# Hybrid decoder layer, input projection: token sums on the vector engine, the rotary turn on GpSimd

## What is computed

```
z = x @ w_in + b_in              # 2048 x 1024 by 1024 x 2240 (parts in the order of the kernel)
# the rotary turn, on the first quarter of each head's columns (16 of 64, or 8 of 32):
x1, x2 = head[:half], head[half:rot]      # half = 8 or 4
x1' = x1*cos - x2*sin ;  x2' = x2*cos + x1*sin
```

## Time and profile before

| | |
|---|---|
| median of 3 runs | 3696.45 us (3692.97 to 3696.48) |
| profiled execution, span from first to last instruction | 3696.2 us |
| mean granted clock of PE | 0.969 |
| PE busy | 3464.1 us (94%) |
| DVE busy | 2404.9 us (65%) |
| ACT busy | 1793.5 us (49%) |
| POOL busy | 1237.3 us (33%) |

### The profile page before, as it was taken

One profiled execution on the slowest core, in us unless ns is written; L12 is line 12 of the kernel. 1 busy time (PEld: TensorE's weight loads), 2 busy tenths in 40 slices (PEclk: granted clock), 3 DMA queues, 4 the chain that ended last, 5 costly groups with the idle time before them and its releaser, 6 DMA issues. The chain is left out here.

```text
span 3696.2 us, 55781 instructions
## 1 busy us (share of the span) xinstructions
PE 3464.1 (94%) x19082; PEld 2965.1 (80%) x19082; DVE 2404.9 (65%) x4983; ACT 1793.5 (49%) x3056; POOL 1237.3 (33%) x1944
## 2 busy tenths in 40 slices
PE   6999978899999999999999899799999999999998
PEld 6999867777888878878878788588888788888876
DVE  9999556667676766676774355756654657665354
ACT  3323235677776777677767333433333333333232
POOL 5454124544443333333222033432321425322021
PEclk9999899899999999999999999899999999999999
DMA  4344310000000000000000245332224442322444
GB/s 146 114 150 146 101 33 24 17 17 24 17 17 10 17 16 9 10 15 5 7 9 27 81 141 155 128 124 79 92 83 171 159 169 77 110 99 89 140 137 171
DMA packets 189701, 289.63 MB, mean 78 GB/s; under 512 B 33395, under 2 KB 129779, under 8 KB 189427
## 3 DMA queue, kind: packets, MB, share of 16 engines
q1 hardware_dynamic: 185300, 285.11, 23.4%
q10 hardware_dynamic: 4128, 1.05, 0.1%
HBM read 211.15 MB, written 74.97 MB: 77 GB/s over the span
## 5 line engine op out<-in xcount | busy, mean ns | idle before, releaser
L1674 ACT ACTIVATE shared<-a_ps_st 128x512 f32<-128x512 f32 x716 | 437.6, 615 | 285.9 <-PE a_ps_st L1560 146.9
L2785 PE MATMUL f_ps<-f_x_four,f_w_hi 128*128 128x512 f32 x1408 | 437.9, 392 | 11.5 <-DVE f_w_lo L2923 11.5
L2785 PE MATMUL f_ps<-f_x_three,f_w_hi 128*128 128x512 f32 x1056 | 325.4, 389 | 1.6 <-DVE f_w_lo L2923 1.6
L2785 PEld LDWEIGHTS f_ps<-f_x_four,f_w_hi 128*128 128x128 f32 x1408 | 266.5, 190 | 68.3 <-DVE f_w_lo L2923 13.1
L1584 PEld LDWEIGHTS a_ps_o<-a_vsl,shared 128*128 128x128 f32 x2176 | 295.5, 200 | 19.3 <-DVE a_fin L1891 0.7
L1382 POOL TENSOR_SCALAR a_tk<-a_tk,a_halves 128x1 f32<-128x1 f32 x336 | 107.0, 318 | 584.1 <-ACT a_junk_a L1681 582.5
L1584 PEld LDWEIGHTS a_ps_o<-a_dv,shared 128*128 128x128 f32 x2176 | 285.9, 194 | 12.0
L1584 PE MATMUL a_ps_o<-a_vsl,shared 128*128 128x65 f32 x2176 | 287.0, 277 | 0.0
L1584 PE MATMUL a_ps_o<-a_dv,shared 128*128 128x65 f32 x2176 | 276.9, 271 | 0.0
L2785 PE MATMUL f_ps<-f_x_four,f_w_lo 128*128 128x512 f32 x704 | 275.8, 392 | 0.0
L294 PE MATMUL p_ps<-pw_hi,px_hi 128*128 128x384 f32 (+1 forms) x672 | 227.9, 339 | 47.3 <-DVE pw_lo L399 29.9
(11 more groups left out here) (372 smaller groups left out, 8905.6 us busy)
## 6 DMA issues: line engine op xcount, KB each, us to landing
shared<-in_w_down SPq DMA_DIRECT2D x88, 512.0 KB, 3.5
px_raw<-in_x_t SPq DMA_DIRECT2D x48, 512.0 KB, 4.6
shared<-in_w_gate SPq DMA_DIRECT2D x44, 512.0 KB, 5.0
shared<-in_w_up SPq DMA_DIRECT2D x44, 512.0 KB, 4.8
g_scratch<-shared SPq DMA_DIRECT2D x22, 1024.0 KB, 7.6
shared<-g_scratch SPq DMA_DIRECT2D x88, 256.0 KB, 3.6
z_scratch<-p_z SPq DMA_DIRECT2D x16, 768.0 KB, 3.4
o_scratch<-a_oacc SPq DMA_DIRECT2D x32, 256.0 KB, 2.1
```

The lines of the kernel that those rows point to most:

```text
L1674: act.activation(p_t[:, s % PT_RING, :], ps_st[s % ST_BANKS][:, :], ACT.Exp, scale=SCALE).then_inc(exp_done, 1)
L2785: mm = pe.matmul(out[:, :], w[:, j, k * P:(k + 1) * P], x_part(j, x)[:, k], start=(k == 0 and i == 0), stop=(k == 3 and i == 2))
```

## The change

The sums of the token blocks of sets 0 and 1 stay on POOL; from set 2 on they are made by DVE, with the same operands, spread over DVE's list: in set `N`, sum 1 of set `N+1` behind slot 0, sum 3 of set `N+1` behind slot 3, sums 0 and 2 of set `N+2` behind slots 5 and 6. Their order within a set changes from 0, 1, 2, 3 to 0, 2, 1, 3, and ACT waits on a new semaphore `sv_done` for them. The rotary turn leaves DVE. POOL makes it for both token tiles of a set at once, in place: two products with `sin` into `rb`, a product with `cos` in `zt` itself (one operation in the first two passes, two in the last), and the sum. To give it operands of few dimensions, the cosines are kept twice side by side (`cos8`) for the heads of 64 and once (`cos4`) for the heads of 32, so ACT makes five tables in place of three. `z_ready` counts one a set in place of two. Small buffers are laid over others, `ra` is gone.

```diff
+        def x_sums(eng, N, k, done, at):
+
+            if k == 3:
+                eng.wait_ge(x_lo_done, SEVEN * N + 2)
+            elif N:
+                eng.wait_ge(x_lo_done, SEVEN * (N - 1) + (4, 3, 7)[k])
+            if k == 0:
+                for half in range(2):
+                    eng.wait_ge(x_ld[2 * (N % 2) + half], 16 * (N // 2 + 1))
+                op = eng.tensor_tensor(s_block(0), x_block(N, 1, 0), x_block(N, 1, 1), ALU.add)
...
         @block.gpsimd
         def _(pool):
...
+            def rope(N):
+
+                a, p = divmod(N, PAIRS_Q)
+                heads, dim, f, fo = ROPES[a]
+                done = 3 * N
+                if N == 0:
+                    pool.wait_ge(trig_done, 5)
+                pool.wait_ge(sum_done, SEVEN * N + 7)
+                if N:
+                    pool.wait_ge(z_ready, N)
+                zr = zt[:, N % 2, :, 0:heads * dim].rearrange("p i (h d) -> p i h d", h=heads)[:, :, :, 0:2 * f]
+                qb = rb[:, :, 0:heads, 0:2 * f]
+                first, second = slice(0, f), slice(f, 2 * f)
+                for m, (dst, src) in enumerate(((first, second), (second, first))):
+                    sn = sin2[:, 2 * p:2 * p + 2, m, fo:fo + f].unsqueeze(2).broadcast_to([P, 2, heads, f])
+                    pool.tensor_tensor(qb[:, :, :, dst], zr[:, :, :, src], sn, ALU.mult).then_inc(turned, 1)
+                pool.wait_ge(turned, done + 2)
+                if fo:
+                    cs = cos4[:, 2 * p:2 * p + 2].unsqueeze(2).broadcast_to([P, 2, heads, f])
+                    pool.tensor_tensor(zr[:, :, :, first], zr[:, :, :, first], cs, ALU.mult)
+                    pool.tensor_tensor(zr[:, :, :, second], zr[:, :, :, second], cs, ALU.mult).then_inc(turned, 1)
+                else:
+                    cs = cos8[:, 2 * p:2 * p + 2].rearrange("p t a f -> p t (a f)").unsqueeze(2).broadcast_to([P, 2, heads, 2 * f])
+                    pool.tensor_tensor(zr, zr, cs, ALU.mult).then_inc(turned, 1)
+                pool.wait_ge(turned, done + 3)
+                pool.tensor_tensor(zr, zr, qb, ALU.add).then_inc(z_ready, 1)
...
             for N in range(NS):
                 a, p = divmod(N, PAIRS_Q)
-                if N + 1 < NS:
-                    x_sums(N + 1)
+                if N == 0:
+                    for k in range(4):
+                        x_sums(pool, 1, k, s_done, 4)
+                if N:
+                    rope(N - 1)
                 if a + 1 < PASSES and 2 <= p <= 5:
                     w_sums(pool, a + 1, p - 2, (t12_done, t12_done, t34_done, t34_done)[p - 2])
+            rope(NS - 1)
...
-                    if j == 1 and N:
-                        rope(N - 1, 0)
-                rope(N, 1)
-            rope(NS - 1, 0)
+                    if j == 0 and 2 <= N + 1 < NS:
+                        x_sums(dve, N + 1, 1, sv_done, 4 * (N - 1))
+                    if j == 3 and 2 <= N + 1 < NS:
+                        x_sums(dve, N + 1, 3, sv_done, 4 * (N - 1))
+                    if j >= 5 and N + 2 < NS:
+                        x_sums(dve, N + 2, (0, 2)[j - 5], sv_done, 4 * N)
```

More of the change, by code:

```diff
@@ L105, in projection_phase @@
         zt = sb("p_z", [P, 2, 2, 2 * WMAX])
[L106 to L109, removed]
+        posi, posf, freq = uu[:, 2, 0:TILES].bitcast(I32), uu[:, 1, 0:TILES], uu[:, 1, TILES:TILES + 12]
+        cos8 = sb("p_cos8", [P, TILES, 2, 8])
+        cos4 = sb("p_cos4", [P, TILES, 4])
         sin2 = sb("p_sin", [P, TILES, 2, 12])
-        ra = sb("p_ra", [P, 12, 2, 8])
-        rb = sb("p_rb", [P, 12, 2, 8])
+        rb = sb("p_rb", [P, 2, 12, 16])
         bank = [ctx.enter_context(nc.psum_tensor(f"p_ps{c}", [P, 512], F32)) for c in range(8)]
@@ L127, in projection_phase @@
         s_done = sem("p_s_done")
+        sv_done = sem("p_sv_done")
         t12_done = sem("p_t12_done")
@@ L143, in projection_phase @@
         z_ready = sem("p_z_ready")
+        turned = sem("p_rope")
         z_out = [sem(f"p_z_out{b}") for b in range(2)]
@@ L205, in store @@
                 a, p = divmod(N, PAIRS_Q)
-                sp.wait_ge(z_ready, 2 * (N + 1))
+                sp.wait_ge(z_ready, N + 1)
                 sp.dma_start(z_rows[:, 2 * p:2 * p + 2, OFFSETS[a]:OFFSETS[a] + 2 * WIDTHS[a]], zt[:, N % 2, :, 0:2 * WIDTHS[a]]).then_inc(z_out[N % 2], 16)
@@ L240, in _ @@
                 sp.wait_ge(z_out[u], 16 * (NS // 2))
+        def x_sums(eng, N, k, done, at):
[7 more added lines that the diff above has]
+                op = eng.tensor_tensor(s_block(0), x_block(N, 1, 0), x_block(N, 1, 1), ALU.add)
+            elif k == 1:
+                op = eng.tensor_tensor(s_block(2), x_block(N, 0, 0), x_block(N, 1, 0), ALU.subtract)
+            elif k == 2:
+                eng.wait_ge(done, at + 1)
+                op = eng.tensor_tensor(s_block(1), s_block(0), x_block(N, 0, 0), ALU.subtract)
+            else:
+                eng.wait_ge(done, at + 3)
+                op = eng.tensor_tensor(s_block(1), x_block(N, 0, 1), s_block(1), ALU.subtract)
+            op.then_inc(done, 1)
@@ L267, in _ @@
             pool.memset(ones[:, :].bitcast(F32), 1.0).then_inc(bias_clear, 1)
-            x_sums(0)
+            for k in range(4):
+                x_sums(pool, 0, k, s_done, 0)
             for n in (2, 3):
@@ L310, in high_x @@
                     act.wait_ge(x_ld[2 * (N % 2) + (j > 0)], 16 * (N // 2 + 1))
+                elif N < 2:
+                    act.wait_ge(s_done, 4 * N + {3: 1, 2: 2, 1: 3, 6: 4}[j])
                 else:
-                    act.wait_ge(s_done, 4 * N + {3: 1, 2: 2, 1: 3, 6: 4}[j])
+                    act.wait_ge(sv_done, 4 * (N - 2) + {3: 1, 1: 2, 2: 3, 6: 4}[j])
                 act.activation(slot(x_hi, j), x_source(N, j), ACT.Copy).then_inc(x_hi_done, 1)
@@ L334, in _ @@
                     act.wait_ge(trig, 1)
-                    act.activation(cos1[:, :, :], rr[:, 1], ACT.Sin).then_inc(trig_done, 1)
+                    for m in range(2):
+                        act.activation(cos8[:, :, m, :], rr[:, 1, :, 0:8], ACT.Sin).then_inc(trig_done, 1)
+                    act.activation(cos4[:, :, :], rr[:, 1, :, 8:12], ACT.Sin).then_inc(trig_done, 1)
                     act.activation(sin2[:, :, 0, :], rr[:, 0], ACT.Sin, scale=-1.0).then_inc(trig_done, 1)
@@ L411, in summed @@
                     dve.wait_ge(first_kept, N + 1)
+                    if N:
+                        dve.wait_ge(sum_done, s0)
                     op = dve.tensor_tensor(u2, m1, piece, ALU.add)
@@ L421, in summed @@
                         dve.wait_ge(z_out[u], 16 * (N // 2))
-                    if N == 0:
-                        dve.wait_ge(trig_done, 3)
                     op = dve.tensor_tensor(zt[:, u, 1, w:2 * w], u3, piece, ALU.add)
@@ L432, in summed @@
                 op.then_inc(sum_done, 1)
[L434 to L452, removed]
             dve.wait_ge(bias_in, 32)
```

## The result

The changed kernel takes 3673.64 us (median of 4 runs, 3666.94 to 3678.91), the kernel before 3694.71 in the runs beside them (3692.89 to 3696.48); with the 3696.45 that stood before the prediction, that is 21 to 23 us less. The ratio is 0.9937, 95% interval 0.9924 to 0.995. The time lies in the range, 3 us under the forecast of 3677. Single executions of one kernel differ by more than that, and with the mean granted clock: the changed kernel's four have spans from 3665.2 us at a clock of 0.973 to 3677.0 at 0.969.

What follows compares the result with a forecast made beforehand. The prediction took PE to bound the last pass and a full DVE, held up by POOL, to keep PE waiting in the first two. -20.4 + 0.6 = -19.8 us gave 3677 us, range 3671 to 3695.

Steps and rivals of the forecast that it cites:

- PE's waits: Projection, sets 1 to 23: 24.7 us are PE waiting or at a lower clock, all that the change can take.
- rival C: Projection: the "issue" waits are PE's own, so 10.1 of the 24.7 us stay, time 3687; chance 0.06.
- DVE's own work: Per projection set: without the rotary turn and with four token sums, 9.9 us, and 9.6 at 352 columns.
- POOL's price for short runs: Rotary turn on POOL: 0.19 us plus 2.16 ns an element, short runs costing nothing extra; 3.2 us in pass 0.
- Rival A: Rotary turn on POOL: short runs are dear, up to 1.43 times, adding 10 to 22 us, time 3687 to 3699; chance 0.16.
- upper bound of 1.43 times: POOL's price an element for short runs: at most about 3.1 ns, from the compare at 1.58 us for 512.
- What POOL holds up: DVE blocked by POOL: 2.3 us a set by the turn (2.1 in pass 1), 2.8 or 3.0 by a weight sum.
- The lag: DVE falls behind PE by 14.9 us at set 15, so PE stops for 4.3 of the 24.7 us: -20.4.
- The room: How far DVE may be behind before PE stops: 11.5 us in pass 0, 10.6 in pass 1.
- The end: Projection's end: POOL's five operations behind the last sum take 2.7 us in place of 2.1, +0.6.
- Sum: Whole kernel: -20.4 + 0.6 = -19.8 us against the span of 3696.2.
- Rival B: Rotary turn on POOL costs twice its price or more: 50 us more over 16 sets, time 3727; chance 0.09.

Runs made afterwards that it cites:

- e2: Changed kernel with the token sums back on POOL for all sets, so only the rotary turn moves; 3678.12 us beside 3703.03 before, ratio 0.9934.
- e4: Changed kernel with four more POOL operations ahead of each rotary turn; projection matmuls end at 394.50, 7.7 us later than in the changed kernel.
- e1: Kernel before with only the token sums moved to DVE from set 2 on; 3694.43 us beside 3703.03 before, ratio 0.998.
- e8: Kernel before with token sums moved to DVE and POOL's weight sums spaced one to a set; 3678.14 us beside 3698.11 before, ratio 0.9947.

## Why the prediction was right

- *PE's waits, 24.7 us to be had.* Right: 344.3 less 320.3 is 24.0 taken. That "issue" was DVE's too (against rival C) is shown: 0.5 is left of 10.1, it is 0 without the turn, and each of the eight stops of before ends 0.10 us after a split of the new weights on DVE. The longest of them, DVE and PE:

```profile
288.63 1.75 DVE L399 TENSOR_TENSOR pw_lo<-shared,pw_hi 128x1536 fp32r<-128x1536 f32 x1
290.48 0.41 PE L294 MATMUL p_ps<-pw_hi,px_hi 128*128 128x384 f32 x1 [2.40 <-issue]
```

- *DVE's own work, 9.9 and 9.6.* Measured 10.0 and 9.7. In the plain set 6 it is idle for 1.0 us, the sign that it has caught up.
- *POOL's price for short runs.* Right: 1.04 us for 384 elements in runs of 16 (1.02 from the line through the earlier trace rows), 1.15 for the two products of 192 in runs of 8 in e2's row above (0.60 forecast for each), and 0.48 for 144 in pass 2 (0.50). Rival A is out: runs of 8 and 16 cost nothing here. The Trainium skill's surcharge ("GPSIMD Engine Reference", Performance pitfalls for Q7 kernels) is put as one on the inner step, and the trace agrees: the jumps between runs don't count as steps. (My upper bound of 1.43 times left the fixed 0.19 us in the compare's 1.58; without it it is 1.26.)
- *What POOL holds up.* The turn 1.9 us for the 2.3 forecast, the weight sum 2.6 for 2.8. The lock of the Trainium skill ("SBUF — State Buffer", Who interferes with whom) agrees with the rows: DVE's low part at 105.22 ends 0.55 us after the POOL operation of 3.70 that began before it.
- *The lag.* This is the term that was mis-sized: 4.3 us of stop forecast, 0.5 found. The mechanism holds, at its place: the only stop is at the change to pass 2, and it ends when DVE has split the last slot's weights. Slot 6 in the trace of after, the last matmul of set 15, DVE's low part and weight split for set 16, and PE's start on it:

```profile
266.50 0.32 PE L325 MATMUL p_ps<-pw_hi,px_lo 128*128 128x352 f32 x1
...
277.73 0.67 DVE L429 TENSOR_TENSOR px_lo<-px_sum,px_hi 128x512 fp32r<-128x512 f32 x1
278.33 1.74 DVE L434 TENSOR_TENSOR pw_lo<-shared,pw_hi 128x1536 fp32r<-128x1536 f32 x1
...
280.17 0.41 PE L325 MATMUL p_ps<-pw_hi,px_hi 128*128 128x384 f32 x1 [0.52 <-issue]
```

DVE is through with slot 6 at 280.07, 13.25 us after PE has left it in set 15 (266.82); less the 1.3 of the sum it is 12.0 behind, for the 14.9 forecast. A set earlier the same measure gives 2.2, for 5.3. So what set 15 adds was right (9.8 for 9.6), and the error lies ahead of it: sets 8 and 9 give back 5.8 us for my 4.2 and the four weight sets add 0.5 each for 0.9, as DVE's periods are 14.4 us in these and 11.5 in a plain set for 14.8 and 11.8. The room was wrong as well: I took that of pass 1, 10.6. But between slot 6 of set 15 and slot 6 of set 16 PE goes through six slots of set 16, which have 384 columns already. Without the stop PE would have started at 279.65, 12.8 us after it left, and the room is 11.5.
- *The end, +0.6.* Measured +0.3.
- *Sum.* -23.9 + 0.3 = -23.6 in the projection for the -19.8 forecast, 3.8 us more, nearly all of it the lag. That the time is 3 us under 3677 fits this but doesn't show it: the four executions lie 12 us apart, and in the profiled one another 3.2 us came from phases that I had at nothing.
- *Rival B's slope.* Wrong by far, though it was not asked for: I priced a longer turn at all its time in 16 sets, and e4 shows a fifth of that.

What I had not seen: which half of the change does it. The prediction took the sum of both, and my first account afterwards, that the sums do it and the turn doesn't matter, fell with e1 and e2. Either half alone gives 19 to 20 us (e2, and e8 with the weight sums spaced), the two together 23.9, because both end at the same ceiling. But moved without the turn the sums gave 8.7, since POOL's waits in its other work had spaced the weight sums, without anyone having meant them to. In the change the turn does this: POOL waits with it for DVE's last sum of each set, and its weight sum stands behind it.

## What to carry to other kernels

Where two engines lock each other out, count what each operation holds up and where the other engine is idle or works from PSUM, not the busy time. Work that is taken off an engine also takes off its waits: what stands behind it in its list may then run in one piece, and it is worth asking what kept it apart. A gain that has a ceiling (here PE's own 319.6 us) is not divided among the parts of a change; test each part alone.

## What the runs showed of the hardware

- DVE's two-input operations and POOL's take turns: in e1, with POOL never idle, each two-input operation of DVE waited for the POOL operation under way and went ahead of the next one, so POOL's sums of 1408 elements took 3.50 to 3.68 us in place of 3.25. An operation of 0.35 us is held up no less than one of 0.68 (they take 3.33 and 3.25): for the work that they do, small two-input operations are the dearest to leave beside long POOL ones.
- One more wait made a kernel faster by 11.4 us of its projection (e8 against e1).
- The rest of the kernel, unchanged, scattered by 12.5 us between single profiled executions (3281.7 to 3294.2), while the start of its set 1 lay within 0.5 us in the eight that share it.
- A stop of PE cost more than its length: behind stops of 3.6 and 7.2 us in e1 the granted clock was 0.50 to the ends of stretches of 6.8 and 10.2 us. In before, five stops of 0.4 to 2.0 us between 161 and 175 brought no such stretch (1.00).
